# Attention in a two-layer decoder trunk: values as the stationary operand in two parts, probabilities scaled before they are turned

## What is computed

```
proj = rms_norm(x) @ w_in                 # q, k, v of 8 + 8 heads, and 8 gate logits
s = q @ k.T / 8 + table_h                 # heads 0-7: -slope*dist + ln(count), heads 8-15: c_t - c_s
p = exp(s - max(s));  o = (p @ v) / sum(p)
x = x + concat(o of 16 heads) @ w_out
```

## Time and profile before

| | |
|---|---|
| median of 3 runs | 1316.77 us (1316.71 to 1316.81) |
| the profiled execution: its own time | 1315.83 us |
| its span, first to last instruction | 1314.0 us |
| granted TensorE clock, mean | 0.998 |
| busy: TensorE, VectorE, ScalarE, GpSimd | 1295.3, 876.9, 703.4, 192.7 us |
| values of the first and the last head begin | 75.16 us, 243.54 us |

### The profile page before, as it was taken

The page is one execution under the profiler, slowest core; times in us unless marked ns, Lnnn a source line. Parts: engine busy times, 40 slices in busy tenths (PEclk is TensorE's granted clock), DMA queues, the critical chain, the costliest instruction groups (busy, mean ns, idle before and its releaser), DMA issues. The chain is left out here.

```text
span 1314.0 us, 18834 instructions
## 1 busy us (share of the span) xinstructions
PE 1295.3 (99%) x7454; PEld 1127.4 (86%) x7454; DVE 876.9 (67%) x1117; ACT 703.4 (54%) x962; POOL 192.7 (15%) x235
## 2 busy tenths in 40 slices
PE   8999999999999999999999999999999999999997
PEld 5788888889798998989888888888879889898995
DVE  5466445468958678598765555555668876959677
ACT  5555445358557464575643433533547646557573
POOL 2131000022111211111101001011021221111220
PEclk9999999999999999999999999999999999999999
DMA  7312221369898988994835735635546898898982
GB/s 253 105 53 68 73 89 57 128 146 238 223 228 175 226 214 219 224 224 135 176 125 128 188 103 117 190 103 112 154 120 154 197 235 220 219 226 193 222 202 92
DMA packets 98056, 215.32 MB, mean 164 GB/s; under 512 B 8489, under 2 KB 25129, under 8 KB 97841
## 3 DMA queue, kind: packets, MB, share of 16 engines
q0 software_dynamic: 24576, 89.68, 35.5%
q1 hardware_dynamic: 73392, 124.44, 29.0%
HBM read 128.09 MB, written 2.11 MB: 99 GB/s over the span
## 5 line engine op out<-in xcount | busy, mean ns | idle before, releaser
L1743 DVE TENSOR_TENSOR w<-raw_tiles,w 128x1024 fp32r<-128x1024 f32 x312 | 371.3, 1221 | 125.4 <-ACT w L1300 125.1
L1300 ACT ACTIVATE w<-raw_tiles 128x1024 fp32r<-128x1024 f32 x312 | 315.0, 1050 | 154.8 <-PE bank L800 63.4
L775 PE MATMUL bank<-h_ops,w 128*128 128x256 f32 x2688 | 324.8, 283 | 0.2
L775 PEld LDWEIGHTS bank<-h_ops,w 128*128 128x128 f32 x2688 | 323.8, 192 | 1.2 <-DVE h_ops L1922 0.6
L800 PE MATMUL bank<-w,arena_q 128*128 128x512 f32 x1344 | 311.0, 391 | 1.8 <-DVE x L1968 1.2
L800 PEld LDWEIGHTS bank<-w,arena_q 128*128 128x128 f32 x1344 | 250.2, 188 | 59.3 <-DVE x L1966 6.1
L2366 POOL DMA_DIRECT2D raw_tiles<-raw_tiles x160 | 138.0, 871 | 648.6 <-DVE w L1743 398.0
L1139 PE MATMUL bank<-w,h_ops 128*128 128x512 f32 x672 | 154.8, 390 | 0.0
L1139 PEld LDWEIGHTS bank<-w,h_ops 128*128 128x128 f32 x672 | 125.6, 188 | 25.8
L1060 PE MATMUL bank<-h_ops,w 128*128 128x512 f32 (+1 forms) x480 | 89.5, 347 | 0.1
L1060 PEld LDWEIGHTS bank<-h_ops,w 128*128 128x128 f32 x480 | 77.3, 189 | 11.8 <-DVE h_ops L1728 0.5
(11 more groups left out here) (165 smaller groups left out, 1438.4 us busy)
## 6 DMA issues: line engine op xcount, KB each, us to landing
raw_tiles<-raw_tiles POOLq DMA_DIRECT2D x160, 512.0 KB, 5.2
raw_tiles<-in_ffn_w_in SPq DMA_DIRECT2D x64, 512.0 KB, 5.9
raw_tiles<-in_ffn_w_out SPq DMA_DIRECT2D x64, 512.0 KB, 5.9
raw_tiles<-in_odd_w_in SPq DMA_DIRECT2D x32, 512.0 KB, 4.4
raw_tiles<-in_even_w_in SPq DMA_DIRECT2D x48, 256.0 KB, 3.2
raw_tiles<-in_odd_w_in SPq DMA_DIRECT2D x32, 256.0 KB, 3.7
raw_tiles<-in_odd_w_out SPq DMA_DIRECT2D x16, 512.0 KB, 4.5
x<-in_x SPq DMA_DIRECT2D x8, 512.0 KB, 6.2
```

The lines of the kernel that those rows point to most:

```text
L775: mm = pe.matmul(bank[first + b][:, 256 * m:256 * m + 256], w_slots[use_slot(use)][:, p, k, c:c + P], h_ops[:, H_BLOCK[op], q, k, :], star ...
L1300: nc.scalar.activation(w_flat(use_slot(use), 0, half), raws[tile][:, 1024 * half:1024 * half + 1024], ACT.Copy).then_inc(m_hi, 1)
L1743: nc.vector.tensor_tensor(w_flat(use_slot(use), 1, half), raws[use_tile(key)][:, 1024 * half:1024 * half + 1024], w_flat(use_slot(use), 0, ...
```

## The change

- The values are split into a high and a low part, side by side, and become the stationary operand (128 columns: 64 high, 64 low). The turned probabilities are also split, and move. A head is eight matmuls, of 512, 384, 256 and 128 columns: four with the high part of the probabilities against all 128 columns, four with the low part against the 64 high ones. The turned blocks are stored in an order (PLACE) in which those of one key block have an even stride.
- The result comes out turned, the two parts in partitions 0 to 63 and 64 to 127 of bank 6 or 7. ScalarE copies the second (output_low), VectorE adds them (output_sum), for every head; the output's transposes go. output_hi and output_lo now read that sum in SBUF.
- Rows are scaled before they are turned: VectorE takes the reciprocals unit by unit (inverse), GpSimd scales the probabilities of heads 0 to 12 in place (prob_scale, four operations a head), VectorE those of heads 13 to 15.
- All three units are copied by ScalarE as the high part (turned_hi), and VectorE makes the low part (turned_lo).
- Value jobs have two copies by ScalarE and two subtractions by VectorE; the bank is free after the latter. The values lie in parts of arena_r and x that are free then.
- The tables of heads 0 to 7 are made on the host and come by DMA from GpSimd's queue, as the bias rows do; the two constants of before are not loaded. The next norm's gain is loaded after attention, since its tile now holds o_sb.

The core of the diff (indented eight less; the other lines are semaphores, arguments and the host's tables):

```diff
@@ -265,17 +265,18 @@
+PLACE = {(0, 0): 0, (1, 0): 2, (2, 0): 4, (3, 0): 6, (1, 1): 1, (2, 1): 5, (3, 1): 9, (2, 2): 3, (3, 2): 7, (3, 3): 8}
+UNIT_PLACE = (6, 3, 0)
+SCALED_BY_POOL = 13
+UNIT_COLS = (512, 384, 384)
+KEY_PLACES = (slice(0, 7, 2), slice(1, 10, 4), slice(3, 8, 4), slice(8, 9, 1))
...
-probT = arena[:, 6656:7936]
+probT = [arena_q[:, o:o + 1280].rearrange("p (b n) -> p b n", n=P) for o in (6656, 8960)]
-delta = arena[:, 8960:9472]
-lncount = arena[:, 9472:9984]
-o_sb = arena[:, 9984:10496]
+o_sb = gain[:, 0:512]
+o_low_sb = gain[0:HD, 512:1024]
-negc = o_sb[0:NFOX, :]
+negc = gain[0:NFOX, 512:1024]
...
+def values_of(group, s):
+    if group == 0:
+        at = 6 if s < 2 else 14
+        part = arena_r[:, at:at + 2, 256 * (s % 2):256 * (s % 2) + 256]
+    else:
+        part = x_q[:, 0:2 * D].rearrange("p (a n) -> p a n", a=2)[:, :, 256 * s:256 * s + 256]
+    return part.rearrange("p a (h n) -> p a h n", h=2)
...
     def turn_prob(h, u):
         q = 3 * h + u
-        pe.wait_ge(prob_ready, 4 * h + (1, 2, 4)[u])
+        if h < SCALED_BY_POOL:
+            pe.wait_ge(prob_normed, 4 * h + (1, 2, 4)[u])
+        else:
+            pe.wait_ge(late_normed, 4 * (h - SCALED_BY_POOL) + (1, 2, 4)[u])
         if q >= 2:
-            pt_wait((q - 2) // 3, (q - 2) % 3)
+            pe.wait_ge(pt_lo, q - 1)
         dst = bank[4 + q % 2]
-        col = 0
         for tb in UNITS[u]:
             for s in range(tb + 1):
-                mm = pe.transpose(dst[:, col:col + P], prob[:, h % 2, OFF[tb] + P * s:OFF[tb] + P * s + P],
+                c = P * (PLACE[tb, s] - UNIT_PLACE[u])
+                mm = pe.transpose(dst[:, c:c + P], prob[:, h % 2, OFF[tb] + P * s:OFF[tb] + P * s + P],
                                   ident[:, :])
-                col += P
         mm.then_inc(ptT_done, 1)
 
     def gather_values(h):
-        if h % 2 == 0 and h >= 2:
-            pe.wait_ge(o_norm, h // 2)
-        pe.wait_ge(aev, e_aev(e_first_job(0 if h < 8 else 4) + 3))
-        for u in range(3):
-            pt_wait(h, u)
-            for tb in UNITS[u]:
-                for s in range(tb + 1):
-                    c = P * tb + HD * (h % 2)
-                    o = OFF[tb] + P * s
-                    mm = pe.matmul(bank[6][:, c:c + HD], probT[:, o:o + P],
-                                   v_sb[:, s, HD * (h % 8):HD * (h % 8) + HD],
-                                   start=(s == 0), stop=(s == tb))
+        pair, head = h // 2, h % 2
+        if h >= 2:
+            pe.wait_ge(o_sum, h - 1)
+        pe.wait_ge(v_lev, 4 if h < 8 else 8)
+        pe.wait_ge(pt_lo, 3 * h + 3)
+        dst = bank[6 + head]
+        for part, rows in ((0, P), (1, HD)):
+            for s in range(TT):
+                v = values_of(pair % 4 // 2, s)[:, pair % 2, head, 0:rows]
+                mm = pe.matmul(dst[0:rows, P * s:S], v, probT[part][:, KEY_PLACES[s], :],
+                               start=(part == 0 and s == 0), stop=(part == 1 and s == TT - 1),
+                               skip_group_check=True)
         mm.then_inc(pv_done, 1)
-
-    def turn_output(pair):
...
@@ -996,9 +994,8 @@
 
         u, what = n // 3, n % 3
         if n == 9:
-            if pair is not None:
-                turn_output(pair)
-        elif what == 0 and h is not None:
+            return
+        if what == 0 and h is not None:
             scores_unit(h, u)
         elif what == 1 and u == 0 and v is not None:
             gather_values(v)
...
             v = prob[:, h % 2, OFF[tb]:OFF[tb] + n]
-            pair, k = h // 2, 2 * tb + h % 2
             nc.scalar.activation(v, v, ACT.Exp, bias=negmax[:, h % 2, c:c + 1], scale=-1.0,
-                                 accum_out=den[:, pair % 2, k:k + 1]).then_inc(prob_ready, 1)
+                                 accum_out=den[:, h % 2, c:c + 1]).then_inc(prob_ready, 1)
+    def output_low(v):
+        act.wait_ge(pv_done, v + 1)
+        if v == 0:
+            act.wait_ge(negc_saved, 16)
+        else:
+            act.wait_ge(o_sum, v)
+        nc.scalar.activation(o_low_sb, bank[6 + v % 2][HD:P, :], ACT.Copy).then_inc(o_low, 1)
 
     def output_hi(pair):
-        act.wait_ge(oT_done, pair + 1)
-        nc.scalar.activation(oT[0][:, pair, :], bank[7][:, :], ACT.Copy).then_inc(oT_hi, 1)
-
-    def copy_turned(g, u):
+        act.wait_ge(o_sum, 2 * pair + 2)
+        nc.scalar.activation(oT[0][:, pair, :], o_sb, ACT.Copy).then_inc(oT_hi, 1)
+    def turned_hi(g, u):
         act.wait_ge(ptT_done, 3 * g + u + 1)
-        o, n = OFF[UNITS[u][0]], (512, 384, 384)[u]
-        nc.scalar.activation(probT[:, o:o + n], bank[4 + (3 * g + u) % 2][:, 0:n],
-                             ACT.Copy).then_inc(pt_s, 1)
+        b, n = UNIT_PLACE[u], UNIT_COLS[u]
+        nc.scalar.activation(probT[0][:, b:b + n // P, :],
+                             bank[4 + (3 * g + u) % 2][:, 0:n].rearrange("p (b n) -> p b n", n=P),
+                             ACT.Copy).then_inc(pt_hi, 1)
 
     def step(h, g, v, pair):
         for u in range(3):
             if h is not None:
                 exps(h, UNITS[u])
-            if g is not None and PT_BY_SCALAR[u]:
-                copy_turned(g, u)
-        if pair is not None:
-            output_hi(pair)
+            if g is not None:
+                turned_hi(g, u)
+            if u == 0 and pair is not None:
+                output_hi(pair)
+            if u == 0 and v is not None:
+                output_low(v)
 
     for n, (kind, i) in enumerate(E_PANELS):
         for q in range(4):
@@ -1509,7 +1516,10 @@
                     act.wait_ge(xn_ready, 2)
                 if i == 1:
                     act.wait_ge(pv_done, 8)
-                nc.scalar.activation(v_sb[:, q, :], bank[e_bank(j)][:, :], ACT.Copy).then_inc(aev, 1)
+                src = bank[e_bank(j)][:, :].rearrange("p (g a h n) -> p g a h n", g=2, a=2, h=2)
+                for group in range(2):
+                    last = nc.scalar.activation(values_of(group, q)[:, :, :, 0:HD], src[:, group], ACT.Copy)
+                last.then_inc(aev, 1)
             if kind == "qk":
                 pair, which = 2 * i + q // 2, q % 2
                 act.wait_ge(job_done, j + 1)
...
@@ -1782,10 +1792,7 @@
         if h == 0 and u == 0:
             dve.wait_ge(negc_ready, 1)
         if u == 0:
-            if h < 8:
-                dve.wait_ge(table_ready, h + 1)
-            else:
-                dve.wait_ge(bias_landed[h % 2], 16 * ((h - 8) // 2 + 1))
+            dve.wait_ge(table_landed[h % 2], 16 * (h // 2 + 1))
         if h >= 2 and u == 0:
             dve.wait_ge(pv_done, h - 1)
         dve.wait_ge(score_done, 3 * h + u + 1)
-    def copy_turned(g, u):
...
-    def normalise(pair):
...
+    def turned_lo(g, u):
+        dve.wait_ge(pt_hi, 3 * g + u + 1)
+        b, n = UNIT_PLACE[u], UNIT_COLS[u]
+        nc.vector.tensor_tensor(probT[1][:, b:b + n // P, :],
+                                bank[4 + (3 * g + u) % 2][:, 0:n].rearrange("p (b n) -> p b n", n=P),
+                                probT[0][:, b:b + n // P, :].bitcast(F32), ALU.subtract).then_inc(pt_lo, 1)
+    def inverse(h, u):
+        dve.wait_ge(prob_ready, 4 * h + (1, 2, 4)[u])
+        c = slice(u, (1, 2, 4)[u])
+        nc.vector.reciprocal(rden[:, h % 2, c], den[:, h % 2, c]).then_inc(rden_ready, 1)
+        if h >= SCALED_BY_POOL:
+            dve.wait_ge(rden_ready, 3 * h + u + 1)
+            for tb in UNITS[u]:
+                v = prob[:, h % 2, OFF[tb]:OFF[tb] + P * (tb + 1)]
+                c = ORDER.index(tb)
+                nc.vector.tensor_scalar(v, v, rden[:, h % 2, c:c + 1], None, ALU.mult).then_inc(late_normed, 1)
+    def output_sum(v):
+        dve.wait_ge(o_low, v + 1)
+        if v >= 2:
+            dve.wait_ge(oT_lo, v // 2)
+        nc.vector.tensor_tensor(o_sb[ROWS[v % 2], :], bank[6 + v % 2][0:HD, :], o_low_sb, ALU.add).then_inc(o_sum, 1)
 
     def output_lo(pair):
         dve.wait_ge(oT_hi, pair + 1)
-        nc.vector.tensor_tensor(oT[1][:, pair, :], bank[7][:, :], oT[0][:, pair, :].bitcast(F32),
+        nc.vector.tensor_tensor(oT[1][:, pair, :], o_sb, oT[0][:, pair, :].bitcast(F32),
                                 ALU.subtract).then_inc(oT_lo, 1)
 
     def step(h, g, v, pair):
         for u in range(3):
             if h is not None:
                 logits(h, u)
-            if g is not None and not PT_BY_SCALAR[u]:
-                copy_turned(g, u)
-        if v is not None and v % 2 == 1:
-            normalise(v // 2)
-        if pair is not None:
-            output_lo(pair)
+            if g is not None:
+                turned_lo(g, u)
+            if h is not None:
+                inverse(h, u)
+            if u == 0 and pair is not None:
+                output_lo(pair)
+            if u == 0 and v is not None:
+                output_sum(v)
 
     for n, (kind, i) in enumerate(E_PANELS):
         for q in range(4):
             j = e_first_job(n) + q
             if kind != "out":
...
     inv_std(0)
```

(91 more changed lines are left out.)

30 lines of the change are left out of this document (5 added, 25 removed).

## The result

| | before | after |
|---|---|---|
| median of the runs | 1316.79 us (1316.71 to 1317.02) | 1348.43 us (1347.2 to 1349.83) |
| profiled execution: its time, its span | 1315.83, 1314.0 us | 1349.83, 1348.0 us |
| granted TensorE clock, mean | 0.998 | 0.985 |
| busy: TensorE, VectorE, ScalarE, GpSimd | 1295.3, 876.9, 703.4, 192.7 us | 1297.2, 900.4, 729.5, 237.4 us |

The ratio of after to before is 1.024, with a 95% interval of 1.0223 to 1.0258: the change costs 31.6 us. The prediction was 1341 with a range of 1318 to 1360. The forecast missed the median by 7.4 us. The sum was made against the profiled execution, and there the end came 9.4 us later than summed (1349.83 to 1340.4).

The account below looks back on a forecast made before the run. In attention VectorE and ScalarE, taking turns, were to bind instead of TensorE: +15.2 us at head 6's values, +12.3 at head 8, +24.6 at the end, on 1315.83 giving 1340.4, said as 1341; range 1318 to 1360.

Parts of the forecast that it names:

- The ring: Attention units: VectorE and ScalarE take turns, their times add; steps grow from 10.3 to about 12.3 us; chance 0.74.
- 3.46 and 0.61: Unit 0 of a step: 3.46 us from its logits on, plus 0.61 for a pair's low part every second step.
- a hold by GpSimd: Before a query tile: GpSimd's last scaling of a head delays VectorE's split, 0.4 us added.
- Logits of head 1 stay at 70.27: Start of attention: the change does not move the logits of head 1, at 70.27 us.
- Behind this TensorE binds again and gains 2.9: After the values of head 6: two value groups and two turned outputs save 2.9 us, +12.3 when head 8 starts.
- 8.25 + 0.95 + 1.4: Last steps, heads 13 to 15: low part at 8.25, VectorE's scaling 0.95, values and handover 1.4; 0.6 more with a pair.
- rival 3: Attention: TensorE's stalls bring its clock down, +17 us on 12 steps, 1358; chance 0.04.
- the likeliest case: Whole kernel: the ring as summed, 1341 us, own range 1331 to 1352.
- Rival 4: New value matmuls: strided moving blocks run at half rate, 1.2 us more a head, +4, 1345; chance within the ring's 0.74.
- the bound of 5 us: Pair's low part on VectorE, reading SBUF alone: held by a GpSimd scaling of 1.49, +5 us.
- Rival 1: Attention: TensorE goes on to bind, needing a ring of about 9 us or less; all 19.6 saved, 1296; chance 0.13.
- Rival 2: Attention: the ring binds but is shorter, 11 us a step, some 1.3 less on 11 steps, 1327; chance 0.07.

Follow-up runs that it names:

- e3: Changed kernel with TensorE's semaphore wait before a head's first scores lowered by one count: 1347.62 us.
- e7: Changed kernel with GpSimd scaling the probabilities of all heads, also the last three: 1346.18 us.
- e8: Kernel before with only its tables brought by DMA as in the change: 1316.25 us.
- e1: Changed kernel with VectorE making the next unit's logits before the present unit's low part: 1312.35 us.
- e11: Changed kernel plus zero matmuls before first scores of full steps (not head 10's), 12 in last steps, 14 before values of head 6: 1343.47 us.
- e5: Changed kernel with VectorE's next logits ahead of the low part, and ScalarE's high part ahead of exp in units 0 and 1: 1304.34 us.
- e4: Changed kernel plus zero matmuls where TensorE waits, 8 before first scores of each full step, 12 in the last steps: 1347.51 us.

## Why the prediction was right, and where its sum was short

**The ring is right, and right in size.** Starts of the 512 wide logits, forecast and measured:

| from head to head | 1-2 | 2-3 | 3-4 | 4-5 | 5-6 | 6-7 | 10-11 | 11-12 | 12-13 | 13-14 | 14-15 |
|---|---|---|---|---|---|---|---|---|---|---|---|
| forecast | 11.2 | 12.4 | 11.8 | 13.0 | 11.8 | 13.0 | 12.4 | 11.8 | 13.0 | 10.6 | 11.2 |
| measured | 10.69 | 12.36 | 11.67 | 13.15 | 11.69 | 13.15 | 12.37 | 11.68 | 13.15 | 11.97 | 12.66 |

In the eight full steps no step is off by more than 0.15. That it fits so well is in part luck, since inside a step errors of both signs meet. In the step of head 4 unit 0 takes 4.27 (111.81 less 107.54), where 3.46 and 0.61 were summed, 0.20 short. From exp to high part it is 0.84, not 0.72, because ScalarE reads its accumulator between them (108.91, shown above). The sum left this read out, though it stands behind every exp before too, as behind that of 119.72 in the earlier trace rows:

```profile
120.35 0.19 ACT L1477 ACTIVATION_READ_ACCUMULATOR arena<-arena,negmax 128x1 f32 x1
```

From the pair's low part to the sum of the halves it is 0.78, not 0.61, and behind the reciprocal 0.06, not 0.15. Unit 1 to unit 2 takes 2.38 (2.36). In the step of head 3, from 95.87 to 107.54, unit 0 is 3.71, 0.25 above its sum, but from ScalarE's split to the next logits it is 3.85 (4.2 was taken, with 0.4 for a hold by GpSimd of which 0.1 came):

```profile
103.69 1.04 ACT L1230 ACTIVATE w<-raw_tiles 128x1024 fp32r<-128x1024 f32 x1
```

**Where the 9.4 us of the profiled execution are.** All from rows, in order:
- *The start, 2.5.* "Logits of head 1 stay at 70.27" failed: they came at 72.82. 2.2 of it stands before the logits of head 0, which came at 63.48 and before at 61.30. The granted clock was 0.60 from 8 to 16 us, where it was 1.00 before. This place moves from execution to execution: in kernels whose start is the same the logits of head 0 came at 60.73 (e3) to 63.86 (e7), and in the kernel before with another table (e8) at 62.92. So it is hardly the change's. In the four traces with a clock of 0.57 to 0.61 from 8 to 16 us they came at 63.07 to 63.86, in the nine with 0.79 at 60.73 to 62.92. The other 0.4 is the change's, and the prediction left it out: from head 0 to head 1 it is 9.34 us, not 8.97, since VectorE waits for each exp before it takes the reciprocal, ahead of the next logits; in e1, where the next logits go first, it is 8.95. The sum of the steps up to head 7 then gave 0.5 back.

```profile
65.07 0.17 DVE L1820 RECIPROCAL rden<-den 128x1 f32<-128x1 f32 x1 [0.89 <-ACT arena L1473]
```

- *Head 7 to the values of head 6, 0.4*: they stand 8.66 behind the logits, not 8.3.
- *Behind the values of head 6, 2.7.* "Behind this TensorE binds again and gains 2.9" failed: from these values to the scores of head 8 it was 22.24 us (136.57 to 158.81), and is 22.04 (154.19 to 176.23), a gain of 0.2. In e11, at full clock there, it is 19.52, a gain of 2.7. The term was right, and the clock took it away. TensorE's rows (the first answers to the earlier trace rows; the last is the values of head 7, at full clock again):

```profile
154.19 2.47 PE L889 MATMUL bank<-arena_q,x_q 128*128 128x512 f32 x8 [3.66 <-DVE arena_q L1813]
156.46 0.73 PE L953 MATMUL bank<-hT_hi,w 128*128 128x512 f32 x1
...
164.72 1.39 PE L889 MATMUL bank<-arena_q,x_q 128*128 128x512 f32 x8
```

- *The last steps, 3.1.* "8.25 + 0.95 + 1.4" gave 10.6 and, with a pair, 11.2; 11.97 and 12.66 were measured, and 9.50 for the last part against 9.2. The 1.4 was values at full clock; they lasted 1.94 and 2.47 us there. In e11 the steps are 11.19 and 11.59, so the clock has 1.85 of it. The rest, 1.3, is there at full clock too: in e11 values follow the logits of heads 13, 14 and 15 by 9.65, 10.06 and 9.50 us, where 9.2, 9.8 and 9.2 were summed, and the next logits come 1.54 and 1.53 later, not 1.4. It isn't the scaling, which makes units 0 and 1 of head 14 in e11 0.85 longer than those of head 4 above (4.67 and 2.83 us, not 4.27 and 2.38), where 0.95 was taken.
- *Behind the values of head 14, 1.2.* The values of head 15 follow 8.60 us later, at a clock of 0.50 from 270 to 275 us, and 6.57 later in e11.

These are 2.5, 0.4, 2.7, 3.1 and 1.2, less 0.5: 9.4.

So the largest part of **what the sum lacked** is that it was made at a clock of 1.00, with its fall put apart as rival 3, which was priced at 17 us as if it had to hold over half of every step. What happened is a small piece of rival 3 beside the ring. In the full steps the clock fell now and then (0.96 from 60 to 140 us) and cost nothing, since a slower TensorE there only shortens its own wait: the steps of heads 2 to 6 are as long in e11, at 1.00, to 0.02 us. Behind the waits at head 6 and in the last steps its work is on the path, and about 5 us were paid (e11). The 2.2 us of the start, nearly a quarter of the 9.4, were most likely chance. The Trainium skill (TensorE: Matmul & The Clock Gate, the section on loop structure) warns of idle waits between bursts; the trace agrees that the lower clock came after TensorE's waits: in 152 to 160 us it was 0.57 behind one of 3.66 us, and 1.00 in e11, where zero matmuls left 0.61 of that wait. By these runs it costs only where TensorE's own time decides.

**The bounds.** The lower bound of the likeliest case, 1331, is not the sum of its terms: 2.5, 1.6 and 1.5 below 1341 are 1335. The upper one, 1352, is. 1348.43 lies between them either way.

**TensorE's idle time.** The prediction said 44 us, "mostly before the value matmuls". It is 33.3, and 17.2 of it before scores. The amount: TensorE's busy time is 1297.2 us, while the same instructions take 1277.9 in e5. 19 us of what would be idle time are filled by matmuls at the lower clock, and busy time can't tell this from work. What it sheds is 17.4 (predicted 19.6). The place is of no account (e3).

**Single terms.** The new values take 1.23 us at full clock (1.22 taken): the values of head 3 start at 104.52 and the projection matmul behind at 105.75. Rival 4, half rate, is out. The reciprocal lasts 0.15, but the next operation begins 0.06 behind it (110.36 to 110.42), and on the ring it is this distance that counts; 0.15 was taken. The split next to GpSimd's scaling lasted 1.33 at 116.98, when plain ones are 1.23: a hold of 0.1 where 0.4 was taken, though GpSimd's two operations ran from 116.75 for 2.02. GpSimd's scaling of a head takes 4.8 us, not 3.8 (1.55, 1.24 and 2.02), hidden as said:

```profile
110.62 1.91 POOL L2379 TENSOR_SCALAR arena<-arena,rden 128x512 f32<-128x512 f32 x1 [3.52 <-DVE rden L1820]
114.37 1.24 POOL L2379 TENSOR_SCALAR arena<-arena,rden 128x384 f32<-128x384 f32 x1 [1.84 <-DVE rden L1820]
116.75 2.02 POOL L2379 TENSOR_SCALAR arena<-arena,rden 128x256 f32<-128x256 f32 x2 [1.15 <-DVE rden L1820]
```

The first is 1.91 beside the pair's low part, which is 0.67 long: the bound of 5 us, VectorE held by GpSimd, did not come. The low part begins 0.06 behind the reciprocal (110.42), GpSimd 0.2 later (110.62), and it is GpSimd that then takes 0.36 longer than alone (1.91 in all three full steps with a pair, 1.55 or 1.56 in the others).

**The rivals.** Rival 1 (TensorE goes on to bind, 1296) is out for the change as it stands, and its condition was named rightly: "if they did not stand ahead of the next logits". e1 took away just this and e5 came to 1304. Rival 2 (a ring of 11 us) is out by the table. Rival 3 holds in part.

## What to carry to other kernels

Where two engines hand a tile to and fro within one unit, and each waits in its own queue before it starts the next unit, their times add, however low their busy shares are; go round the ring operation by operation and set the sum against the engine that bounds now. If it is longer, put the next unit's first operation ahead of the present unit's last one: two lines of order were worth 36 us here, over twice what TensorE had been relieved of. And once TensorE has to wait, price its lower clock only where its own work decides.

## What was not expected of the hardware

- Busy time hides a low clock: with the same instructions TensorE showed 1297.2 us at a mean clock of 0.985 and 1277.9 at 0.997.
- More work made the kernel faster: 5.0 us less with zero matmuls in the waits (e11), the clock going from 0.57 to 1.00 in the stretch behind the longest wait.
- VectorE's split beside a scaling by GpSimd (one tensor input) that had begun 0.23 before it was hardly held, 1.33 instead of 1.23, while in the kernel before a split beside GpSimd's operation on two tensors, of which 1.16 us were still to run, took 2.25. Why the two differ is open.
- What stays open: why the clock was at 0.60 from 8 to 16 us in this execution and not in the one of the kernel before. It differs between executions whose start is the same; no run was made to settle it. As to e4, expected at −4 to −8 and come to −0.9: e11 differs from it in two places alone, and their distances in the traces give each its part, 1.75 us at head 10 (15.99 to 14.24 from head 9) and 2.4 behind head 6 (31.44 to 29.06 from head 7 to head 8), together the 4.0 between the two medians.
